# PEER mixture layers: where ScalarE copies the later quarters' gates, and how VectorE lays out its second-key one-hots

## The chip, the cores and the metric

One core of one Trainium2 chip runs the whole program. The metric is the device time of one execution in microseconds; the kernel before takes 3299.89 us (median of 3 runs, 3299.41 to 3300.56).

## The reference

Two transformer blocks in float32, one after the other, over 512 tokens of width 1024. Each has a mixer (gated linear attention in the first; retention and stick-breaking attention in the second) and then a PEER layer, and the change lies in the PEER layers alone:

```python
q = (ht @ w_query).reshape(T, 8, 2, 128)            # 8 heads, two halves
sub_scores = einsum('thpc,hpkc->thpk', q, sub_keys) # 128 keys in each half
top_s, top_i = top_k(sub_scores, 16)
cand = top_s[:, :, 0, :, None] + top_s[:, :, 1, None, :]
best_s, best_c = top_k(cand.reshape(T, 8, 256), 16)
expert_id = top_i[first] * 128 + top_i[second]      # one of 16384 experts
gate = softmax(best_s)
a = einsum('pd,ped->pe', x, expert_down[expert_id])
y = einsum('pe,ped->pd', gelu(a) * gate, expert_up[expert_id])
```

Each token so picks 128 experts (8 heads of 16), each with one row of a "down" table and one of an "up" table, 16384 x 1024 float32 each.

## The kernel before

The 512 tokens are four tiles of 128. Tiles 0 and 1 are gathered: GpSimd fetches each picked row with an indirect DMA (`fetch`, L2038) into rings of six buffers; VectorE multiplies and sums down rows (`score_rows`, L1843, its work on L1850) and adds up rows (`add_rows`, L1854, its work on L1870). Four rows for all 128 tokens are a unit. Tiles 2 and 3 are dense: the whole tables stream through SBUF in 128 blocks of 128 experts, one block for each value e of the first key. For block e TensorE computes the first product (`first_product`, L744, matmul on L750: 128 experts x 256 tokens), ScalarE the gelu of it (`block_gelu`, L1203, on L1208), VectorE multiplies two blocks by their gates (`weigh_pair`, L1793, on L1801), and TensorE accumulates the second product (`second_product`, L754, on L760). SyncE loads the blocks, four ahead, as the buffers come free.

The gates of the dense tiles are a table of experts x tokens, mostly zeros. They are built for four quarters of the first key in turn (32 values each), 256 tokens in 64 batches of 4 tokens for each quarter. For one batch, `gates_of_batch` (L770, matmuls on L786) multiplies a one-hot of the second key (128 picks x 128 keys for each token: `hits`, four buffers, in the memory called `levels`) with a one-hot of the first key times the gate in three bf16 parts (`hot`, in `x`): 12 matmuls of 128x32. The second-key one-hots come from ScalarE (`hit_batch`, L1210: four ACTIVATE on L1218, one on L1221) for all batches but the odd ones of the first quarter, which VectorE makes (`second_keys`, L1783, on L1789). `by_scalar` (L81) says which. VectorE makes the first-key side for 16 tokens at a time (`first_keys`, L1769, on L1777 and L1779). When 16 tokens (4 batches, one bank of PSUM; two banks take turns) are done, ScalarE copies the bank into the gate table in SBUF (`copy_gates`, L1223, on L1228).

The order of the work is written out by hand, for each engine in steps e = 0 to 127, and each engine runs strictly in its order. TensorE's step e (`dense_experts`, L800): first product of block e + 16 (from e = 8; the first 24 lie in the stage before), second product of e, then gate batches `batches_due(e - 1)` to `batches_due(e)` of the quarters 1 to 3. Before the steps stands the first quarter, with blocks 8 to 23 between its batches. ScalarE's step e is this:

```python
for u in range(units_due(e - 2), units_due(e - 1)):
    unit_gelu(layer, u)
if EARLY <= e + AHEAD - 1 < NKEY:
    block_gelu(layer, e + AHEAD - 1)
for n in range(batches_due(e) if e else 0, batches_due(e + 1)):
    hit_batch(layer, 1 + n // BATCHES, n % BATCHES)
for m in range(copies_due(e - 1), copies_due(e)):
    copy_gates(layer, 1 + m // WIDES, m % WIDES)
```

EARLY is 24 and AHEAD 16. First product e waits for the gelu of e - 2 (two banks). A copy waits for its four batches and for VectorE to have weighed the two blocks whose place it takes; a group of batches waits for the copy of the group two before it. VectorE's step e weighs blocks e + 4 and e + 5 if e is even, makes first-key sides up to `spreads_due(e)`, does a piece of the choice of experts for tile 1, and runs the units that a planner (`unit_table`) gives to the step.

Of the kernel before, what the change touches and what calls it, by code (L numbers as in the profile page):

```python
# [8 lines left out]
BF16 = mybir.dt.bfloat16  # L9
U32 = mybir.dt.uint32  # L10
I32 = mybir.dt.int32
ALU = mybir.AluOpType
# [3 lines left out]
P = 128  # L16
# [13 lines left out]
QA = NKEY // QUARTERS  # L30
UV = 4
BATCH = 4
# [9 lines left out]
HITS = 4  # L42
# [38 lines left out]
def by_scalar(q, n):  # L81

    return q > 0 or n % 2 == 0


def scalar_batches(layer, q, n):

    return sum(by_scalar(a, b) for a in range(QUARTERS) for b in range(BATCHES)) * layer \
        + sum(by_scalar(a, b) for a in range(q) for b in range(BATCHES)) + sum(by_scalar(q, b) for b in range(n))


def vector_batches(layer, q, n):

    return (layer * QUARTERS + q) * BATCHES + n - scalar_batches(layer, q, n)
# [7 lines left out]
LATER = (QUARTERS - 1) * BATCHES  # L102


def batches_due(e):

    return 0 if e < 0 else min(LATER, 2 * e + 4 + min(8, e // 4))
# [6 lines left out]

def copies_due(e):

    return 0 if e < 0 else min(LATER // 4, e // 2 + 3, batches_due(e + 1) // 4)


def blocks_before(n):  # L120
# [89 lines left out]
def build(nc, a, out, mod_dram, x_dram, two_pi):  # L210
    with ExitStack() as ctx:
        def sb(name, cols, dt=F32):
            return ctx.enter_context(nc.sbuf_tensor(name, [P, cols], dt))[:, :]
# [5 lines left out]
        ps = [psum[:, n * 512:(n + 1) * 512] for n in range(8)]  # L219
# [10 lines left out]
        modm = sb("mod", 6 * D)  # L230
# [8 lines left out]
        def part(base, at_kib, kib, dt=F32):  # L239
            v = base[:, int(at_kib * 256):int((at_kib + kib) * 256)]  # L240
            return v if dt == F32 else v.bitcast(dt)
# [25 lines left out]

        onehot = part(modm, 16, 3, BF16)
        wide_onehot = part(x_, 8, 4, BF16)
        row_at, row_to = part(modm, 16, 0.5), part(modm, 16.5, 0.5)  # L270
        cand = part(modm, 17, 0.5).rearrange("p (h n) -> p h n", h=2)
        place_no = part(modm, 19, 1, BF16).rearrange("p (k s) -> p k s", k=TOPK)
# [35 lines left out]
        second_no = part(hT_, 14, 0.5, BF16)  # L308
        hits = [part(lev_, b, 1, BF16) for b in range(HITS)]
# [47 lines left out]
        keyno16 = sb("key_numbers_16", P // 2).bitcast(BF16)  # L357
# [273 lines left out]
        def _(pe):  # L631
# [138 lines left out]
            def gates_of_batch(layer, q, n):  # L770

                m = (layer * QUARTERS + q) * WIDES + n // 4
                if by_scalar(q, n):
                    pe.wait_ge(hit_ready, scalar_batches(layer, q, n + 1))
                else:
                    pe.wait_ge(hit_by_vector, vector_batches(layer, q, n + 1))
                if n % 4 == 0:
                    pe.wait_ge(ga_ready, m + 1)
                    if q == 0 and n < 8:
                        pe.wait_ge(picks_copied, len(DENSE) * (layer + 1))  # L780
                    else:
                        pe.wait_ge(ga_copied, m - 1)
                for j in range(BATCH):
                    t = n % 4 * BATCH + j
                    for r in range(3):
                        last = nc.tensor.matmul(ps[6 + n // 4 % 2][:, t * QA:(t + 1) * QA], hits[n % HITS][:, j * P:(j + 1) * P],  # L786
                                                hot[n // 4 % 2][:, r, n % 4, :, j], start=r == 0, stop=r == 2)
                last.then_inc(ga_used, 1)

# [10 lines left out]
            def dense_experts(layer):  # L800

                for n in range(BATCHES):
                    gates_of_batch(layer, 0, n)
                    for e in range(blocks_before(n), blocks_before(n + 1)):
                        first_product(layer, e)
                for e in range(NKEY):
                    if EARLY <= e + AHEAD < NKEY:
                        first_product(layer, e + AHEAD)
                    second_product(layer, e)
                    for n in range(batches_due(e - 1), batches_due(e)):  # L810
                        gates_of_batch(layer, 1 + n // BATCHES, n % BATCHES)
                if layer == 0:
                    pe.wait_ge(x_ready, NT)
# [22 lines left out]
            for i in range(ALONE + 1):  # L836
                chunk(i)
                if i == 1:
                    pe.wait_ge(cst_in, 16 * 13)
                    for k in range(KC):  # L840
                        last = nc.tensor.matmul(ps[4][0:16, :], w_low[:, k, :], hT[:, k, :], start=k == 0, stop=k == KC - 1)
                    last.then_inc(low_done, 1)
                if i == 2:
                    seen.next(low_copied)
                    for c in range(2):
                        last = nc.tensor.matmul(ps[5 + c], w_up[:, c * P:(c + 1) * P], glow, start=True, stop=True)
# [93 lines left out]
            for h in range(8):  # L940
                prt = heads[h % 2]
                for j in range(NT):
                    n = h * NT + j
# [21 lines left out]
            for n in range(STICKS + LOOK):  # L965
                if n < STICKS:
                    h, j = n // NT, NT - 1 - n % NT
# [4 lines left out]
                if m >= 0:  # L972
                    h, j = m // NT, NT - 1 - m % NT
# [5 lines left out]
                    for i in range(NT - 1, j - 1, -1):  # L979
                        last = nc.tensor.matmul(bank[:, (i - j) * P:SEQ - j * P], sticks[:, 0 if i == j else 1, :],  # L980
                                                stay[h % 2][:, i, i * P:SEQ], start=False, stop=i == j)
# [12 lines left out]
        def _(act):  # L994
# [260 lines left out]
            def dense_acts(layer):  # L1255
# [16 lines left out]
                for e in range(NKEY):  # L1272
# [8 lines that stand above are left out]
                    if e and pieces_due(e - 2) <= EXP_PIECE < pieces_due(e - 1):  # L1281
                        gate_exp(1)
                    if layer == 0 and e and units_due(e - 2) < 2 * GROUPS + 1 <= units_due(e - 1):
                        seen.next(x_ready)
                        squares(0)
# [78 lines left out]
        def _(dve):  # L1364
            seen, step, chosen = Seen(dve), Chain(dve, c_dve), Chain(dve, c_top)
            picks, spreads = Chain(dve, c_picks), Chain(dve, c_first)
            n_out = [0]
            tt, ts, stt = nc.vector.tensor_tensor, nc.vector.tensor_scalar, nc.vector.scalar_tensor_tensor

            def spread(v, shape):  # L1370

                while len(v.shape) < len(shape):
                    v = v.unsqueeze(len(v.shape))
                return v.to_broadcast(shape)
# [200 lines left out]
            def by_head(v, n, width):  # L1575
                return v.rearrange("p (h n) -> p h n", n=width), [P, n, width]
# [5 lines left out]
            for t in range(NT):  # L1582
                hv, shape = by_head(hn[:, t, :], 8, P)
                step(tt(hv, hv, spread(rs[:, t * 8:t * 8 + 8], shape), ALU.mult))
                for m in range(2):
# [3 lines left out]
                    last = tt(half, half, sg1[:, m, t, :], ALU.mult)  # L1589
# [142 lines left out]
            def peer(layer):  # L1732
# [22 lines left out]
                finish_gates(0)  # L1755
                for g in range(WIDE // BATCH):
                    spreads(nc.vector.tensor_copy(key_rows[:, g], spread(keyno[:, 0:QA], [P, QA, BATCH])), 3)
                dve.wait_ge(picks_copied, len(DENSE) * (layer + 1))
                for q in range(QUARTERS):
                    spreads(ts(first_no[q], iaT, float(-q * QA), None, ALU.add), 3)  # L1760
# [22 lines left out]
                def second_keys(n):  # L1783

                    at = layer * QUARTERS * BATCHES + n
                    if at >= HITS:
                        dve.wait_ge(ga_used, at - HITS + 1)
                    shape = [P, BATCH, P]
                    tt(hits[n % HITS].rearrange("p (j k) -> p j k", j=BATCH), keyno16.unsqueeze(1).to_broadcast(shape),  # L1789
                       second_no[:, n * BATCH:(n + 1) * BATCH].unsqueeze(2).to_broadcast(shape), ALU.is_equal)\  # L1790
                        .then_inc(hit_by_vector, 1)

                def weigh_pair(e):  # L1793
# [10 lines left out]
                for n in range(BATCHES):  # L1804
                    if n % 4 == 0:
                        first_keys(0, n // 4)
                    if not by_scalar(0, n):
                        second_keys(n)
                    for u in range(first_units(n - 1), first_units(n)):
                        run_unit(layer, u)  # L1810
# [63 lines left out]
            def finish_tile(layer, t, y):  # L1874
# [6 lines left out]
                else:  # L1881
# [3 lines left out]
                    dve.wait_ge(out_ready, t + 1)  # L1885

            peer(0)
            dve.sem_inc(dve_to_act, 1)

# [40 lines left out]
            for m in range(2):  # L1930
                for t in range(NT):
# [8 lines left out]
                    r3, shape = by_head(r, 8, 64)  # L1940
# [5 lines left out]
            for h in range(8):  # L1946
# [3 lines left out]
                for j in range(NT):  # L1950
                    n = h * NT + j
# [24 lines left out]
            for n in range(STICKS + LOOK):  # L1976
# [3 lines left out]
                if n in (3, 6, 9, 12):  # L1980
                    seen.next(ss_done)
                    t = n // 3 - 1
# [6 lines left out]
                if n < STICKS:  # L1989
                    h, j = n // NT, NT - 1 - n % NT  # L1990
# [13 lines left out]
                if m >= 0:  # L2004
                    h, j = m // NT, NT - 1 - m % NT
# [13 lines left out]
            for t in range(NT):  # L2019
# [7 lines left out]
                rstd(1, D, t)  # L2027
                normed_tile(t, rows[:, 1, :], mod[:, 3, :])
            peer(1)


# [59 lines left out]
```

## Time and profile before

| | |
|---|---|
| median of 3 runs | 3299.89 us (3299.41 to 3300.56) |
| profiled execution | 3302.15 us, span 3300.2 us |
| mean granted TensorE clock | 0.973 |
| TensorE (matmul) busy | 3081.3 us, 93% |
| VectorE busy | 2418.4 us, 73% |
| ScalarE busy | 1338.2 us, 41% |
| GpSimd busy | 1304.0 us, 40% |
| DMA | 931.21 MB, mean 282 GB/s |

The span goes from the first to the last instruction; the execution's own time is 2 us longer. The two PEER layers' steps run from about 560 to 1570 us and from about 2240 to 3300 us. Engine names in the rows: PE is TensorE's matmul, PEld its weight load, DVE VectorE, ACT ScalarE, POOL GpSimd, SP SyncE. `L1208` is a line of the kernel.

### The profile page before, as it was taken

How to read it: one execution, taken by the hardware profiler on the slowest of the kernel's cores; microseconds unless marked ns; L12 is line 12 of the kernel's file. 1: busy time of each engine (PE TensorE's matmuls, PEld its weight loads, DVE VectorE, ACT ScalarE, POOL GpSimd, SP SyncE). 2: the span in 40 equal slices, each digit the busy share in tenths (PEclk: the TensorE clock that was granted, in tenths of full speed). 3: DMA queues.
4: the chain of work that ended last, by engine and by line, in shares of the span. 5: the costliest groups of instructions: out<-in, count | busy, mean ns of one | idle time of the engine just before them, and what ended most of it. 6: DMA issues, size and time to landing. Idle time of an engine off the chain costs nothing. (4 is left out here: it accounts for less than half of the span.)

```text
span 3300.2 us, 45872 instructions
## 1 busy us (share of the span) xinstructions
PE 3081.3 (93%) x16440; PEld 2052.6 (62%) x16440; DVE 2418.4 (73%) x5311; ACT 1338.2 (41%) x3417; POOL 1304.0 (40%) x1040
## 2 busy tenths in 40 slices
PE   7999899889999999999799999998899999999999
PEld 2466478756666666666344565687666666666664
DVE  5874459989889887877721243499898898888767
ACT  3232112676566555500101153126765656555100
POOL 0000000656665766666200000005465566777554
PEclk9999999999999999999899989999999999999999
DMA  8510252989999999999812101428899999999998
GB/s 293 193 42 36 96 209 79 339 291 395 379 380 395 403 409 409 409 409 409 314 56 83 36 35 39 179 77 296 283 391 375 370 398 400 409 408 409 409 409 336
DMA packets 282681, 931.21 MB, mean 282 GB/s; under 512 B 31804, under 2 KB 32460, under 8 KB 281944
## 3 DMA queue, kind: packets, MB, share of 16 engines
q0 software_dynamic: 147840, 536.96, 41.7%
q1 hardware_dynamic: 134616, 391.34, 31.4%
q8 instruction: 131, 2.15, 0.3%
q14 instruction: 94, 0.77, 0.1%
HBM read 921.87 MB, written 6.32 MB: 281 GB/s over the span
## 5 line engine op out<-in xcount | busy, mean ns | idle before, releaser
L750 PE MATMUL psum<-hT,mod 128*128 128x256 f32 x4096 | 966.7, 391 | 57.4 <-ACT big L1208 48.1
L750 PEld LDWEIGHTS psum<-hT,mod 128*128 128x128 f32 x4096 | 780.2, 195 | 182.9 <-issue 80.7
L1218 ACT ACTIVATE levels<-key_numbers,hT 128x128 bf16<-128x128 f32 x1792 | 566.9, 389 | 104.8 <-PE psum L786 104.0
L1870 DVE SCALAR_TENSOR_TENSOR tmp<-w,small,tmp 128x1024 f32<-128x1024 f32 x339 | 435.7, 1285 | 88.6 <-DMA w<-in_peer_v,tmp 43.5
L2045 POOL DMA_INDIRECT w<-in_peer_u,tmp x172 | 230.9, 1343 | 582.9 <-DVEq L1699 447.2
L1850 DVE CUSTOM_DVE_ANT_0 w<-w,hn 128x1024 f32<-128x1024 f32 x342 | 408.0, 1223 | 69.4 <-DMA w<-in_peer_u,tmp 33.9
L2045 POOL DMA_INDIRECT big<-in_peer_down,tmp x86 | 117.3, 1363 | 714.7 <-DVEq L1699 647.8
L760 PE MATMUL psum<-rows,big 128*128 128x512 f32 x768 | 343.9, 592 | 0.0
L786 PEld LDWEIGHTS psum<-x,levels 128*128 128x128 bf16 x6144 | 225.6, 101 | 170.0 <-issue 104.9
L1228 ACT ACTIVATE big<-psum 128x512 f32<-128x512 f32 x128 | 137.2, 1072 | 399.9 <-PE psum L786 390.1
L786 PE MATMUL psum<-x,levels 128*128 128x32 bf16 x6144 | 237.0, 196 | 54.9 <-DVE levels L1789 31.1
L1221 ACT ACTIVATE levels<-levels 128x512 bf16<-128x512 bf16 x448 | 282.2, 630 | 14.2
L2045 POOL DMA_INDIRECT w<-in_peer_down,tmp x170 | 225.9, 1329 | 143.6 <-DVE small L1850 102.7
L2045 POOL DMA_INDIRECT w<-in_peer_v,tmp x172 | 210.3, 1223 | 109.6 <-DVE tmp L1870 67.0
L1870 DVE SCALAR_TENSOR_TENSOR tmp<-big,small,tmp 128x1024 f32<-128x1024 f32 x169 | 217.2, 1285 | 43.8 <-DMA big<-in_peer_up,tmp 22.3
L2045 POOL DMA_INDIRECT w<-in_peer_up,tmp x170 | 203.1, 1195 | 115.0 <-DVE tmp L1870 76.0
L760 PEld LDWEIGHTS psum<-rows,big 128*128 128x128 f32 x768 | 145.9, 190 | 149.5 <-issue 145.4
L1850 DVE CUSTOM_DVE_ANT_0 big<-big,hn 128x1024 f32<-128x1024 f32 x170 | 203.8, 1223 | 30.1 <-DMA big<-in_peer_down,tmp 15.1
L1234 ACT ACTIVATE small<-small 128x4 f32<-128x4 f32 x128 | 26.0, 203 | 458.0 <-DVE small L1850 458.0
L760 PE MATMUL psum<-srow,big 128*128 128x512 f32 x384 | 172.6, 592 | 0.0
L760 PE MATMUL psum<-tmp,big 128*128 128x512 f32 x384 | 172.6, 592 | 0.0
L737 PE MATMUL psum<-hT,w 128*128 128x256 f32 x640 | 144.8, 379 | 0.0
(328 smaller groups left out, 4186.8 us busy)
## 6 DMA issues: line engine op xcount, KB each, us to landing
mod<-in_uT SPq DMA_DIRECT2D x256, 512.0 KB, 6.8
rows<-in_peer_v SPq DMA_DIRECT2D x64, 512.0 KB, 6.8
rows<-in_peer_up SPq DMA_DIRECT2D x64, 512.0 KB, 6.8
w<-in_w_in SPq DMA_DIRECT2D x14, 2048.0 KB, 7.8
srow<-in_peer_v SPq DMA_DIRECT2D x32, 512.0 KB, 7.0
tmp<-in_peer_v SPq DMA_DIRECT2D x32, 512.0 KB, 6.9
srow<-in_peer_up SPq DMA_DIRECT2D x32, 512.0 KB, 6.8
tmp<-in_peer_up SPq DMA_DIRECT2D x32, 512.0 KB, 6.9
```

The source lines that it names most:

```text
L737: last = nc.tensor.matmul(bank[:, 0:2 * P], w[:, k, c * P:(c + 1) * P], hT[:, k, tokens], start=k == 0, stop=k == KC - 1)
L750: last = nc.tensor.matmul(ps[4 + e % 2][:, 0:ND], ub[e % UV][:, k, :], hT[:, k, ND:SEQ], start=k == 0, stop=k == KC - 1)
L760: last = nc.tensor.matmul(y_dense[n][:, c * 512:(c + 1) * 512], zg(e)[:, n * P:(n + 1) * P], vb[e % UV][:, c * 512:(c + 1) * 512], start=e ...
L786: last = nc.tensor.matmul(ps[6 + n // 4 % 2][:, t * QA:(t + 1) * QA], hits[n % HITS][:, j * P:(j + 1) * P], hot[n // 4 % 2][:, r, n % 4, : ...
L1218: last = nc.scalar.activation(hits[n % HITS][:, j * P:(j + 1) * P], keyno, ACT.Abs, bias=nibT[:, n * BATCH + j:n * BATCH + j + 1])
L1221: nc.scalar.activation(hits[n % HITS], hits[n % HITS], ACT.Relu, scale=-1.0, bias=1.0).then_inc(hit_ready, 1)
L1228: nc.scalar.activation(gates[q % 2][:, :, 2 * m:2 * m + 2, :], ps[6 + m % 2].rearrange("p (j i a) -> p a j i", a=QA, i=8), ACT.Copy).then_ ...
L1234: nc.scalar.activation(g8[g % 2], a8[g % 2], ACT.Gelu).then_inc(act_out, 1)
L1850: nc.vector.tensor_tensor_reduce(out=row, in0=row, in1=hn[:, g // GROUPS, :], scale=1.0, scalar=0.0, op0=ALU.mult, op1=ALU.add, accum_out= ...
L1870: last = stt(y, row, c8[g % 2][:, b:b + 1], y, ALU.mult, ALU.add)
L2045: nc.gpsimd.indirect_dma_start(ring[n % ROWS], None, table, bass.IndirectOffsetOnAxis(idx[:, c:c + 1], 0))\
```

## The change

It does two things. The count of copies that ScalarE may have done by step e is taken from the batches of step e instead of e + 1. And VectorE's second-key one-hots, for the odd batches of the first quarter, are written key by key with the four tokens innermost, where they were token by token with the 128 keys innermost; for this a grid of key numbers, each four times, is written once in each layer, and TensorE reads the weights of these batches with a step of four elements.

```diff
 def copies_due(e):
-    return 0 if e < 0 else min(LATER // 4, e // 2 + 3, batches_due(e + 1) // 4)
+    return 0 if e < 0 else min(LATER // 4, e // 2 + 3, batches_due(e) // 4)
...
+        key_grid = part(modm, 16, 1, BF16).rearrange("p (k j) -> p k j", j=BATCH)
...
+                rows_of = "p (j k) -> p j k" if by_scalar(q, n) else "p (k j) -> p j k"
+                hit = hits[n % HITS].rearrange(rows_of, j=BATCH)
                 for j in range(BATCH):
                     t = n % 4 * BATCH + j
                     for r in range(3):
-                        last = nc.tensor.matmul(ps[6 + n // 4 % 2][:, t * QA:(t + 1) * QA], hits[n % HITS][:, j * P:(j + 1) * P],
+                        last = nc.tensor.matmul(ps[6 + n // 4 % 2][:, t * QA:(t + 1) * QA], hit[:, j, :],
                                                 hot[n // 4 % 2][:, r, n % 4, :, j], start=r == 0, stop=r == 2)
...
+                spreads(nc.vector.tensor_copy(key_grid, spread(keyno16, [P, P, BATCH])), 4)
...
-                    shape = [P, BATCH, P]
-                    tt(hits[n % HITS].rearrange("p (j k) -> p j k", j=BATCH), keyno16.unsqueeze(1).to_broadcast(shape),
-                       second_no[:, n * BATCH:(n + 1) * BATCH].unsqueeze(2).to_broadcast(shape), ALU.is_equal)\
+                    tt(hits[n % HITS].rearrange("p (k j) -> p k j", j=BATCH), key_grid,
+                       second_no[:, n * BATCH:(n + 1) * BATCH].unsqueeze(1).to_broadcast([P, P, BATCH]), ALU.is_equal)\
                         .then_inc(hit_by_vector, 1)
```

LATER is 192, the batches of quarters 1 to 3, and `batches_due(e)` is min(192, 2e + 4 + min(8, e // 4)).

## Rows read from the trace of the kernel before

**Rows 1.** The page: TensorE's busy line, and the chain that ended last.

```profile
PE 3081.3 (93%) x16440; PEld 2052.6 (62%) x16440; DVE 2418.4 (73%) x5311; ACT 1338.2 (41%) x3417; POOL 1304.0 (40%) x1040
...
DMA 9%; PE 2%; DVE 2%; POOL 2%; issue 1%; DVEq 0%; ACT 0%; POOLq 0%; ACTq 0%
```

**Rows 2.** Windows: from:to, length, busy time per engine, granted clock, DMA share, GB/s.

```profile
589.00:692.00 103.00, 86.52 (x1005) 75.13 (x1006) 100.57 (x174) 73.11 (x185) 67.65 (x52) 0.92 0.94 347
...
758.00:950.00 192.00, 177.51 (x1133) 122.76 (x1134) 162.74 (x358) 110.39 (x301) 113.59 (x91) 1.00 0.99 381
950.00:1100.00 150.00, 150.00 (x932) 102.54 (x931) 144.54 (x283) 94.02 (x249) 100.15 (x79) 1.00 1.01 394
1100.00:1500.00 400.00, 390.88 (x2189) 265.96 (x2188) 314.62 (x440) 176.06 (x479) 271.29 (x210) 0.99 1.03 409
2258.00:2361.00 103.00, 84.88 (x1009) 73.71 (x1010) 100.27 (x173) 73.22 (x186) 68.48 (x52) 0.95 0.95 351
...
2427.00:2620.00 193.00, 178.52 (x1131) 123.34 (x1130) 162.04 (x358) 109.71 (x299) 112.98 (x90) 0.99 0.98 376
2620.00:2800.00 180.00, 180.00 (x1123) 123.61 (x1122) 168.65 (x317) 111.79 (x297) 119.90 (x96) 1.00 1.02 398
```

**Rows 3.** Durations (ns, min/median/max) of L1789, L1777 and L1757, both layers.

```profile
L1789 DVE TENSOR_TENSOR levels<-key_numbers,hT x64: 680/689/693, 589.1 to 2359.5; 128x512 bf16<-128x512 bf16 x64
...
L1777 DVE TENSOR_TENSOR x<-x,hT x128: 405/421/448, 587.6 to 3059.9; 128x512 bf16<-128x512 bf16 x128
...
L1757 DVE CAST x<-key_numbers x8: 215/222/250, 583.7 to 2252.8; 128x128 bf16<-128x128 f32 x8
```

**Rows 4.** TensorE's waits (us, times, longest), first quarter of layer 1, then layer 2.

```profile
PE psum L786 <- DVE levels L1789: 14.9, 8, 2.9
PE psum L786 <- ACT levels L1221: 5.4, 3, 4.5
...
PE psum L786 <- DVE levels L1789: 16.2, 9, 2.2
```

**Rows 5.** Timeline of TensorE: first and last of L750's waits, each layer.

```profile
757.90 3.69 PE L750 MATMUL psum<-hT,mod 128*128 128x256 f32 x16 [1.49 <-ACT big L1208]
...
946.32 3.69 PE L750 MATMUL psum<-hT,mod 128*128 128x256 f32 x16 [1.09 <-ACT big L1208]
...
2426.67 3.69 PE L750 MATMUL psum<-hT,mod 128*128 128x256 f32 x16 [1.49 <-ACT big L1208]
...
2616.76 3.69 PE L750 MATMUL psum<-hT,mod 128*128 128x256 f32 x16 [1.09 <-ACT big L1208]
```

**Rows 6.** Timeline around one such wait: start, length, engine, line, [idle before].

```profile
790.08 0.93 PE L786 MATMUL psum<-x,levels 128*128 128x32 bf16 x24
...
790.66 1.05 ACT L1228 ACTIVATE big<-psum 128x512 f32<-128x512 f32 x1 [6.18 <-PE psum L786]
...
791.57 0.38 ACT L1208 ACTIVATE hT<-psum 128x256 f32<-128x256 f32 x1
791.84 1.27 ACT L1218 ACTIVATE levels<-key_numbers,hT 128x128 bf16<-128x128 f32 x4
...
792.10 3.69 PE L750 MATMUL psum<-hT,mod 128*128 128x256 f32 x16 [1.09 <-ACT hT L1208]
```

**Rows 7.** VectorE's waits: two rows of 760 to 1000, one of 950 to 1565.

```profile
DVE x L1777 <- PE psum L786: 20.2, 9, 4.2
DVE big L1801 <- ACT big L1228: 5.1, 1, 5.1
...
DVE tmp L1870 <- DMA w<-in_peer_v,tmp: 38.9, 49, 1.8
```

**Rows 8.** Weight loads: L786's durations, one batch in the timeline, L750's group.

```profile
L786 PEld LDWEIGHTS psum<-x,levels x6144: 95/101/117, 589.2 to 3080.5; 128*128 128x128 bf16 x199
...
654.11 0.54 PE L786 MATMUL psum<-x,levels 128*128 128x32 bf16 x12
...
L750 PEld LDWEIGHTS psum<-hT,mod 128*128 128x128 f32 x4096 | 780.2, 195 | 182.9 <-issue 80.7
```

## The prediction

> **What bounds the kernel now.** I read the page first. TensorE is busy 93% of the span, VectorE 73%, and the chain that ended last names DMA before any engine [rows 1]. So no single engine is the answer, and the stages have to be taken apart. The windows do that for the two mixture layers, which have the same shape [rows 2]. Four stretches matter in each.
>
> First quarter of the gates (589 to 692 us, and 2258 to 2361): VectorE is busy 100.6 of 103 us, TensorE 86.5. DMA moves 347 GB/s, under the 409 it reaches later. VectorE never waits here. TensorE does: 14.9 us in the first layer and 16.2 in the second on the one-hots of L1789, and some more on ScalarE's [rows 4]. VectorE is the bound, and the instruction TensorE waits for is the one that the diff rewrites.
>
> Later quarters, first part (758 to 950, and 2427 to 2620): TensorE is busy 177.5 of 192 us. Its gaps are all of one kind: L750, the first product of a block, waits for the gelu L1208. There are 13 such gaps in each layer, the first at 757.90 and the last at 946.32 in the first layer, 15.9 us together (0.69 to 1.49 each); in the second layer 13 from 2426.67 to 2616.76, 16.0 us [rows 5]. One of them in full [rows 6]: TensorE's gate products begin at 790.08; the copy L1228, which had waited 6.18 us for them, starts at 790.66 and takes 1.05 us; only behind it, in ScalarE's order, comes the gelu at 791.57, and the first product starts at 792.10, 1.09 us late.
>
> Then 950 to 1100: TensorE is busy all the time, at 394 GB/s. From 1100 to 1500 the queues move a flat 409 GB/s and VectorE waits for landed rows again and again (38.9 us on one form alone, 49 times, from 950 to the layer's end, none of it before 950) [rows 2, 7]. That last stretch is bound by DMA: it starts earlier if what is ahead of it ends earlier, but does not get shorter.
>
> **The change, part by part.**
>
> Copies. ScalarE's step e ends with the copies that `copies_due(e)` newly allows. Before, that was a batch count of step e+1 over 4; after, of step e. TensorE runs the gate batches up to `batches_due(e)` at its step e, after the second product. So before, a copy at ScalarE's step e could wait for the end of TensorE's step e+1, and the gelu of step e+1 behind it is wanted by TensorE at the start of its step e+2, that is, at once. I wrote out both functions for e = 0 to 127: they differ at e = 1, 3, 5, 7, 8, 10, 12, 14, 15, 17, 19, 21, 23, 24, 26, 28 and 30, so 17 of the 48 copies of a layer move one step later. From e = 32 on the other bound, e // 2 + 3, holds in both. First products lie beside second products only from e = 8: of the 17, that leaves 13, and two steps on from them comes a pattern of gaps 2, 2, 2, 1, 2, 2, 2, 2, 1, 2, 2, 2 steps. The 13 waits of the trace are spaced just so (two steps are about 17 us, one about 9.6). Each of these waits is one moved copy.
>
> After the change, the copy waits for TensorE's step e, and the gelus needed at its steps e+1 and e+2 are issued before it and one step behind it, 7 us before they are wanted. So all 15.9 and 16.0 us of gaps should go from TensorE. What moves behind other work is only the copy: ahead of it now stand the row gelus of a unit, one block gelu and 2 or 3 one-hot batches (1.27 us each on L1218 [rows 6] and a shorter pass on L1221), of which at most the last can still be running when TensorE ends its step. That makes a copy up to 2 us later than the products allow. TensorE needs the bank again only a group later, over 7 us on: covered. At a quarter's end VectorE waits for its last copy (5.1 us, once in a layer [rows 7]); that may grow to 7 us, beside 20.2 us that VectorE waits for TensorE in the same stretch: nothing. No DMA issue of SP or POOL is moved; both follow TensorE's and VectorE's progress.
>
> What is late next is DMA. From 758 to 1100 it moves 192 x 381 + 150 x 394 = 132,250 (us x GB/s). At 409 that takes 323 us, at 394 (what it reached while rows were already waited for) 336 us, against 342: the stretch can lose between 6 and 18.6 us, capped by the 15.9 of the gaps. Middle of 6 and 15.9: 11 us. In the second layer 193 x 376 + 180 x 398 = 144,210, which is 353 us at 409 and 362 at 398, against 373: between 10.7 and 16.0, middle 13 us. **Copies: 24 us** together (ends 17 and 32).
>
> One-hots. L1789 takes 689 ns for 128x512 bf16 with a stride of 0 innermost in one operand. The new form has both operands and the output with a unit stride innermost over four tokens, and the key dimension broadcast outside it. L1777, same operation, size and types, same pattern of its second operand, takes 421 ns [rows 3]. 32 instructions in each layer save 268 ns each: 8.6 us. Added is one copy of 512 elements per layer to fill the key grid, between 0.22 us (L1757, 128 elements) and 0.69 us; I take 0.5, in full, as TensorE's first gate batch waits for VectorE's chain there. That is 8.1 us a layer. VectorE fills this stage to 98%, so it counts in full, up to TensorE's own need (86.5 busy of 103, part of it at a granted clock of 0.92 [rows 2]). DMA would have to rise from 347 to 377 GB/s. **One-hots: 16 us** together; ends 0 (rows become the wait) and 20 (the gaps of ScalarE's one-hots shrink as well).
>
> The weights of TensorE's gate products now lie four elements apart in the odd batches of the first quarter: 384 loads in a layer. No row shows such a load. A batch of 12 loads and matmuls takes 0.54 us with the pipeline's fill, 24 take 0.93, so about 36 ns a pair; the moving operand is already read at that stride. The record of one load is 101 ns, that of an f32 load 195 [rows 8]. So the price lies between 0 and (195 - 36) x 384 = 61 us a layer, a gain being excluded because nothing gets denser. I take 0, from the moving operand. At 101 ns a pair it would be 25 us, of which some 20 are idle time of TensorE now.
>
> The Trainium skill (TensorE: Matmul & The Clock Gate, Weight-path perf modes) says that a fast weight load reads 32 bits at a time, two bf16 weights, which speaks against this change: two neighbours of the new order are not in one such word. The same table lists the read pattern as "packed or strided", which speaks for no cost. No row shows which holds, so the first reading is rival 5.
>
> **Sum.** 24 + 16 = 40 us from the profiled execution's 3302.15 us (span 3300.2): 3262. The median shown is 2.3 us lower, so 3260 us.
>
> **Rivals.**
> 1. DMA gives back most of the copies' gain. VectorE runs into row waits as soon as TensorE stops holding it, and the 409 GB/s stretch just starts with a longer backlog. For it: the margins above are 3% to 5%. Against: at 409 GB/s the first layer's rows 2 leave 16 us of DMA unused in the first quarter and 19 from 758 to 1100. Only the one-hots count: 3300 - 16 = 3284; with a little of the copies, 3276 to 3293. Chance 0.16.
> 2. More than forecast: all 32 us of gaps, 16 of one-hots, and some 8 us from a higher granted clock and fewer waits for ScalarE's one-hots. 3300 - 56 = 3244. Chance 0.12.
> 3. Slower: strided weight loads set TensorE's pace in the first quarter. Place: L786 in odd batches. It eats TensorE's 20 us of waits first, then works against the copies' 12 us: it decides from 32 / 384 = 83 ns over the present pair, near 120 ns. At the f32 load's 195 ns, 61 - 20 - 12 = 29 us a layer, 58 us more: 3358. Chance 0.05.
> 4. No change: both gains only turn into longer row waits, 3300. If DMA were the bound from the stage's start this would hold, but VectorE waits for no row before 950. Chance 0.06.
> 5. A strided pair takes twice as long, 72 ns for 36: 14 us a layer on TensorE, beside 20 us of its waits there. It costs the one-hots' gain at most, 3276. Chance 0.05. The Trainium skill's 32-bit reads, taken strictly, are this case.
>
> **How the numbers follow.** My own case, 3250 to 3275, has 0.56; with rivals 1, 2 and 5 that is 0.89 below 3293. A difference within 0.2% (6.6 us) is about what a measurement of this kernel cannot tell from none: 3293 to 3306, 0.06. Above: 0.05. The range reaches from rival 2 to most of rival 1: 3242 to 3288.
>
> **What would show it.** L1789's successor at about 421 ns, x64. The 13 waits of L750 for L1208 gone in both layers, and the copies still starting at the end of gate products but with no gelu queued behind. The first quarter down from 103 to about 95 us, L786's waits for it cut. TensorE's loads in odd batches still about 36 ns a pair. From 758 on, DMA near 400 GB/s, with VectorE's first row waits before 950. I am wrong if the stage after 1100 starts less than 12 us earlier in the first layer, if it starts earlier but ends no earlier, or if 12-matmul batches of L786 take over 1 us.

## The result and the profile after

The changed kernel takes 3254.49 us (median of 4 runs, 3254.21 to 3257.26), against 3300.22 us before on the same chip: a ratio of 0.986, interval 0.9848 to 0.9871, or 43 to 50 us. Forecast were 3260 us and a range of 3242 to 3288.

Both parts do what the diff says. The one-hots, from the view of single lines in the kernel after (duration min/median/max in ns), beside [rows 3]:

```profile
L1792 DVE TENSOR_TENSOR levels<-mod,hT x64: 417/422/427, 589.7 to 2329.3; 128x512 bf16<-128x512 bf16 x64
L1781 DVE TENSOR_TENSOR x<-x,hT 128x512 bf16<-128x512 bf16 x128 | 53.8, 420 | 15.9 <-PE psum L789 15.5
L1761 DVE COPY mod<-key_numbers x2: 412/416/419, 584.5 to 2229.6; 128x512 bf16<-128x512 bf16 x2
```

The second is the group of L1781, the old L1777: its twin to 2 ns. The third is the added key grid, 0.42 us a layer. TensorE's batches with the new stride of the weights take 0.57 to 0.58 us where they stand alone, against 0.54 to 0.56 before and 0.54 for the unchanged batches of the same kernel; one of them:

```profile
628.67 0.58 PE L789 MATMUL psum<-x,levels 128*128 128x32 bf16 x12 [2.01 <-DVE levels L1792]
```

The windows of the kernel after, the columns as in [rows 2]:

```profile
589.70:683.70 94.00, 80.46 (x980) 71.02 (x981) 91.69 (x174) 73.25 (x185) 67.43 (x51) 0.98 0.99 375
763.00:950.00 187.00, 187.00 (x1221) 129.07 (x1220) 171.57 (x377) 119.92 (x321) 127.60 (x97) 1.00 1.03 408
950.00:1100.00 150.00, 150.00 (x923) 102.88 (x922) 138.53 (x261) 86.09 (x223) 100.62 (x76) 1.00 1.01 397
1100.00:1500.00 400.00, 385.32 (x2087) 261.50 (x2086) 313.65 (x436) 165.99 (x450) 272.60 (x211) 0.99 1.03 409
2235.00:2330.00 95.00, 83.93 (x988) 73.53 (x989) 91.66 (x173) 73.01 (x185) 66.47 (x51) 0.95 0.98 373
```

The first quarter is down from 103 to 94 us with VectorE as full as before. The granted clock rose there in layer 1, from 0.92 to 0.98, and TensorE's busy time fell from 86.5 to 80.5 us; its idle time fell only from 16.5 to 13.5 us. But the stage is VectorE's, and in layer 2, where the clock stayed at 0.95, it got shorter as well. From 763 to 950 TensorE has no gap left, and DMA moves 408 GB/s where it moved 381. TensorE's waits in layer 1, first in the kernel before, then in the kernel after (us, times, longest):

```profile
PE psum L750 <- ACT big L1208: 23.2, 14, 4.6
PE psum L786 <- DVE levels L1789: 14.9, 8, 2.9
PE psum L786 <- ACT levels L1221: 10.3, 9, 4.5
PE psum L750 <- ACT hT L1208: 3.6, 3, 1.5
```

```profile
PE psum L751 <- ACT big L1211: 16.1, 7, 6.5
PE psum L789 <- DVE levels L1792: 13.3, 8, 2.0
PE psum L789 <- ACT levels L1224: 7.8, 4, 4.9
PE psum L751 <- ACT hT L1211: 1.3, 1, 1.3
```

The 13 waits of [rows 5] are gone. The waits for VectorE's one-hots are cut less: 14.9 to 13.3 us here, 16.2 to 10.3 in layer 2. The seven and one that L751 still has all come after 1140 us, the longest at 1194. They are of another kind, as the timeline there shows (idle before, in brackets):

```profile
1192.38 1.23 DVE L1853 CUSTOM_DVE_ANT_0 big<-big,hn 128x1024 f32<-128x1024 f32 x1 [0.69 <-DMA big<-in_peer_u,tmp]
...
1193.65 0.21 ACT L1237 ACTIVATE small<-small 128x4 f32<-128x4 f32 x1 [11.06 <-DVE small L1853]
1193.76 0.37 ACT L1211 ACTIVATE big<-psum 128x256 f32<-128x256 f32 x1
1194.27 5.38 PE L751 MATMUL psum<-hT,mod 128*128 128x256 f32 x16 [6.49 <-ACT big L1211]
```

ScalarE stands at the gelu of a unit, which VectorE has not scored because the rows land late, and the block's gelu stands behind it. This is where DMA takes back part of what the gaps gave: waits of this kind add up to 17.4 us in layer 1 and 16.9 in layer 2, where the kernel before has 10.9 and 13.5. VectorE's first waits for rows now lie before 950 us, where it had none; the longest group of them, from 560 to 950:

```profile
DVE tmp L1873 <- DMA w<-in_peer_v,tmp: 4.9, 13, 0.8
```

A copy in the kernel after, to be laid beside [rows 6]:

```profile
771.79 0.37 ACT L1211 ACTIVATE hT<-psum 128x256 f32<-128x256 f32 x1
...
774.72 0.93 PE L789 MATMUL psum<-x,levels 128*128 128x32 bf16 x24
...
775.49 3.70 PE L751 MATMUL psum<-hT,mod 128*128 128x256 f32 x16
775.72 1.07 ACT L1231 ACTIVATE big<-psum 128x512 f32<-128x512 f32 x1
776.58 0.42 ACT L1211 ACTIVATE hT<-psum 128x256 f32<-128x256 f32 x1
```

The gelu that the product at 775.49 wants was done at 772.2, before the copy. A gelu follows the copy still, at 776.58, but it is the next step's. The copy starts 1.0 us after the gate products began, 0.4 us later than in [rows 6], because one-hots stand before it: the "up to 2 us" of the prediction, and nobody waits for it.

Where the time went, from first and last starts of single lines in the traces (us; block 12 is the first whose second product reads its gelus from `big`, which the trace tells apart, at 778.5 us before and 763.2 after in layer 1):

| stretch | before, layer 1 / 2 | after | copies only | one-hots only | 4 early copies | 13 late copies |
|---|---|---|---|---|---|---|
| first gate product to last VectorE one-hot | 101.6 / 101.5 | 93.5 / 94.3 | 101.5 / 101.6 | 93.9 / 94.2 | 101.5 / 101.6 | 101.5 / 101.5 |
| to block 12's second product | 87.7 / 87.8 | 79.9 / 81.9 | 81.8 / 81.9 | 87.8 / 87.8 | 85.1 / 85.2 | 84.4 / 84.5 |
| to the last gate product | 632.8 / 633.2 | 622.0 / 621.1 | 621.6 / 621.2 | 636.7 / 633.8 | 634.7 / 634.9 | 621.6 / 622.0 |

The three stretches give 52 us together. The trace after is only 48 us shorter: the time from the last gate product to the last second product grew by 0.9 us in layer 1, that from there to layer 2's first gate product by 2.2 us, and the time ahead of layer 1's first gate product by 0.6. Apart from the key grid (0.42 us a layer, which lies ahead of the first gate product), the change touches nothing there. Yet the time between the layers is 636.2 to 637.1 us in all six traces of this document with the old one-hots, 639.2 to 640.0 in six of the eight with the new ones, and 636.9 and 637.4 in the other two. So some 2 us of the one-hots' gain seem to be lost there; by what is not shown.

### The profile page after: what moved, and what is told of

Its sections match the earlier page's. It is cut to its first block and busy times, and to the rows that moved or that the text cites. A ratio compares the mean times of both kernels' runs of the same rounds, so it can differ in the third digit from the quotient of the medians.

```text
span 3252.1 us, 45874 instructions
## 1 busy us (share of the span) xinstructions
PE 3070.5 (94%) x16440; PEld 2047.1 (63%) x16440; DVE 2400.6 (74%) x5313; ACT 1347.2 (41%) x3417; POOL 1339.4 (41%) x1040
## 5 line engine op out<-in xcount | busy, mean ns | idle before, releaser
L751 PE MATMUL psum<-hT,mod 128*128 128x256 f32 x4096 | 957.9, 388 | 35.4 <-ACT big L1211 32.1
L751 PEld LDWEIGHTS psum<-hT,mod 128*128 128x128 f32 x4096 | 773.9, 193 | 156.4 <-issue 57.1
L761 PE MATMUL psum<-rows,big 128*128 128x512 f32 x768 | 343.9, 592 | 0.0
L789 PEld LDWEIGHTS psum<-x,levels 128*128 128x128 bf16 x6144 | 227.5, 103 | 152.9 <-issue 102.7
L789 PE MATMUL psum<-x,levels 128*128 128x32 bf16 x6144 | 236.3, 196 | 40.1 <-DVE levels L1792 23.6
L2048 POOL DMA_INDIRECT w<-in_peer_v,tmp x172 | 218.1, 1268 | 98.4 <-DVE tmp L1873 54.3
L2048 POOL DMA_INDIRECT w<-in_peer_up,tmp x170 | 211.7, 1246 | 99.1 <-DVE tmp L1873 57.9
L761 PEld LDWEIGHTS psum<-rows,big 128*128 128x128 f32 x768 | 145.9, 190 | 149.6 <-issue 145.4
L761 PE MATMUL psum<-srow,big 128*128 128x512 f32 x384 | 172.6, 592 | 0.0
L761 PE MATMUL psum<-tmp,big 128*128 128x512 f32 x384 | 172.6, 592 | 0.0
```

The costliest lines, as they stand in the source:

```text
L751: last = nc.tensor.matmul(ps[4 + e % 2][:, 0:ND], ub[e % UV][:, k, :], hT[:, k, ND:SEQ], start=k == 0, stop=k == KC - 1)
L761: last = nc.tensor.matmul(y_dense[n][:, c * 512:(c + 1) * 512], zg(e)[:, n * P:(n + 1) * P], vb[e % UV][:, c * 512:(c + 1) * 512], start=e ...
L2048: nc.gpsimd.indirect_dma_start(ring[n % ROWS], None, table, bass.IndirectOffsetOnAxis(idx[:, c:c + 1], 0))\
```

## Experiments

The kernel before takes 3300 us on the chips of the first comparison and of the first four experiments, and 3350 to 3352 us on the chips of the other eight runs. So each kernel is held against the kernel before, or after, on its own chip.

**Each half alone, and the copies split in two.** From the kernel before, the first with the new `copies_due` only, the second with everything but it, and two that change it for some steps:

```diff
 e3: only steps before 8
-    ... batches_due(e + 1) // 4)
+    ... batches_due(e if e < 8 else e + 1) // 4)
 e4: only steps from 8 on
+    ... batches_due(e if e >= 8 else e + 1) // 4)
```

> The copies' half alone: later quarters' gates copied a step later, one-hots as before. Theory (two separate gains that add): 45.7 us less some 16 us of one-hots, so 30 us faster than before, near 3270 us; L750's 13 waits in each layer gone, L1789 still 689 ns. Rival (DMA is the common limit and each half alone would reach it): over 36 us faster, under 3264 us, and the two halves' gains sum to well over 46. Second rival (most of the gain is the one-hots'): 3285 us or more.

> The one-hots' half alone, copies as before. Theory: 8 us a layer, near 3284 us, with the first quarter's stage at about 94 us and L750's 13 waits a layer still there. Rival (common limit): 22 us or more faster. Second rival (VectorE's time turns into waits of the later stage): less than 8 us faster.

> Only the 4 copies of each layer before step 8 are moved (those of steps 1, 3, 5 and 7), nothing else. My prediction costed them at nothing: within 3 us of before. Rival: the stretch from the end of the first quarter to the first product's pairing got shorter by more than the 3 us of L750's two waits in it, so these four copies hold back ScalarE's one-hots: 3 to 5 us a layer, 6 to 10 us faster.

> Only the 13 copies of each layer from step 8 on are moved. Theory: all of the copies' gain, 28 to 32 us faster. Rival (DMA gives back a third and the early copies pay for it): 20 to 25 us faster. All 26 waits of L750 for the gelu gone in both cases, so what is missing from 32 us must show as VectorE's waits for rows or as later waits of L750.

| kernel | median us | ratio to before (interval) | gain us (interval) |
|---|---|---|---|
| before | 3301.19 | | |
| copies only | 3267.79 | 0.9899 (0.9883 to 0.9915) | 33 (28 to 39) |
| one-hots only | 3290.70 | 0.9962 (0.9946 to 0.9978) | 13 (7 to 18) |
| 4 early copies a layer | 3295.90 | 0.9984 (0.9975 to 0.9994) | 5 (2 to 8) |
| 13 late copies a layer | 3271.89 | 0.9913 (0.9897 to 0.9928) | 29 (24 to 34) |

The gains are worked out from the ratios; by the medians the one-hots alone win 10.5 us. Within these intervals the gains add: 33 and 13 are 46, the gain of the whole, and 5 and 29 are 34, for the 33 of the copies. The rival of a common limit falls: it wanted 22 us or more from the one-hots alone. So does the one that gives most to the one-hots, with 3285 us or more for the copies alone.

The early copies were costed at nothing (within 3 us) and are worth 5 us, between that and the rival's 6 to 10. TensorE's waits in layer 1 with only them moved:

```profile
PE psum L750 <- ACT big L1208: 24.2, 15, 4.6
PE psum L786 <- DVE levels L1789: 14.7, 8, 2.9
PE psum L786 <- ACT levels L1221: 8.3, 6, 4.5
```

The same waits for ScalarE's one-hots in the stretch to block 12 alone (690.8 to 778.5 us before, 688.2 to 773.3 with the early copies moved):

```profile
PE psum L786 <- ACT levels L1221: 4.9, 6, 1.3
```

```profile
PE psum L786 <- ACT levels L1221: 3.0, 3, 1.3
```

These 1.9 us are most of the 2.6 us by which the stretch gets shorter in each layer; the rest was not traced. In steps 0 to 7 TensorE has no first products, its steps mostly last 4 to 6 us, and ScalarE makes 2 or 3 one-hot batches in each. In the kernel before, ScalarE stands for TensorE at a copy in their midst (2.74 us at 716 us), with one-hots behind it:

```profile
715.16 0.93 PE L786 MATMUL psum<-x,levels 128*128 128x32 bf16 x24
...
716.13 1.08 ACT L1228 ACTIVATE big<-psum 128x512 f32<-128x512 f32 x1 [2.74 <-PE psum L786]
716.99 1.24 ACT L1218 ACTIVATE levels<-key_numbers,hT 128x128 bf16<-128x128 f32 x4
```

The late copies bring 29 of the 32 us of gaps. Two of the 13 gaps, 3.0 us, lie before block 12 (the stretch is 3.3 us shorter), the other eleven (13.0 us) shorten the next stretch by 11.2. DMA gives back little. The one-hots alone win 7.5 us in the first quarter of each layer and lose 3.9 and 0.6 before the last gate product. But the traced execution is the slowest of its seven (3296.41 us, the others from 3279.34), so that this loss may be the spread of the runs. L751 still has its waits there, 25.6 us in layer 1; that VectorE's lead only waits behind them is argued, not shown.

**All weight loads strided.** From the kernel after, ScalarE writes its one-hots in the new order too:

```diff
-                    last = nc.scalar.activation(hits[n % HITS][:, j * P:(j + 1) * P], keyno, ACT.Abs,
+                    last = nc.scalar.activation(hits[n % HITS].rearrange("p (k j) -> p j k", j=BATCH)[:, j, :], keyno, ACT.Abs,
...
-                rows_of = "p (j k) -> p j k" if by_scalar(q, n) else "p (k j) -> p j k"
+                rows_of = "p (k j) -> p j k"
```

> The kernel after, with ScalarE's one-hots laid out by key and then token as well, so that all 3072 gate weight loads of a layer, not 384, step over four elements. Theory (a strided load costs TensorE nothing): a batch of 12 still starts and ends in 0.54 to 0.55 us, pairs at 36 ns, and the whole is within 6 us of the changed kernel, near 3255 us. Rival (the load loses half its rate, 36 ns more a pair): 2688 more such loads a layer where TensorE is busy all the time, 97 us a layer, near 3440 us. A slower ScalarE write at this stride would show in L1218's successor, now 389 ns.

3273.73 us, a ratio of 0.9763 (0.974 to 0.9786) to before; the kernel after, on another chip where before also takes 3351 us, has 0.9765. So no time is lost that this interval, 8 us to either side, would show. The loads, then a step's 24 pairs, then ScalarE's writes:

```profile
L789 PEld LDWEIGHTS psum<-x,levels x6144: 110/118/135, 592.4 to 3059.9; 128*128 128x128 bf16 x199
...
1003.90 0.95 PE L789 MATMUL psum<-x,levels 128*128 128x32 bf16 x24
...
L1221 ACT ACTIVATE levels<-key_numbers,hT x1792: 532/553/622, 587.9 to 3050.2; 128x128 bf16<-128x128 f32 x200
```

One load's record is 118 ns instead of 101, but 24 pairs take 0.95 us instead of 0.93: about 1 ns a pair. The rival at half the load rate wanted 36 ns a pair and 3440 us, and falls. ScalarE, though, pays: 553 ns a write of 128 elements instead of 388. It has room for it here.

**DMA relieved.** The kernels before and after with half of each down block loaded, so that the products use stale values for the rest. The edit, the same in both:

```diff
-                sp.dma_start(ub[e % UV], layer_uT[layer][:, e * D:(e + 1) * D].rearrange("p (k n) -> p k n", k=KC))\
+                sp.dma_start(ub[e % UV][:, 0:KC // 2, :], layer_uT[layer][:, e * D:e * D + D // 2].rearrange("p (k n) -> p k n", k=KC // 2))\
```

> The kernel before with only half of each down block loaded (the first 4 of its 8 slices; the products use stale values in the rest), which takes 33.5 MB, 82 us at 409 GB/s, from each layer's queues and nothing from any engine. Theory (DMA binds after 1100 us only): the stretch from 1100 on gets shorter by what TensorE and VectorE wait for rows there, 10 to 40 us in all; the 26 waits of L750 stay. Rival (DMA binds everywhere): near 160 us less. It is the base for the next run.

> The kernel after with the same half loads. Theory (DMA gives back a few us of the gain, no more): the difference to the half-loaded kernel before is 45 to 56 us, a little above the 46 of the full kernels. Rival (DMA was what held the gain down, and the gaps of TensorE were worth more): over 60 us. Second rival (with DMA relieved the gaps were covered by something else): under 35 us.

3333.26 us (0.9934 of before, 0.9911 to 0.9958) and 3248.40 us (0.9685, 0.966 to 0.971): 85 us apart, outside the 45 to 56 of the theory. Against 46 us that would have spoken for the rival "DMA held the gain down". But the kernel before took 3352 us on this chip, so the sizes could not be compared before the next runs. What can be read by itself: relieved of 164 us of transfers (an estimate: 67 MB at the 409 GB/s of [rows 2]), the kernel before gains 19 us by the medians, 14 to 30 by the interval, so DMA does not bind everywhere. And in the half-loaded kernel after L751's waits for ScalarE are gone from layer 1 altogether (its whole list for L751, L761 and L789):

```profile
PE psum L789 <- issue: 10.3, 18, 1.6
PE psum L789 <- ACT levels L1224: 7.4, 3, 4.9
PE psum L789 <- DVE levels L1792: 6.2, 5, 1.6
...
PE psum L751 <- issue: 1.0, 3, 0.4
PE psum L761 <- DVE x L1804: 0.2, 1, 0.2
```

The full kernel after, on a chip where before also takes 3351 us (it comes next), still has them:

```profile
PE psum L751 <- ACT big L1211: 6.3, 3, 2.9
PE psum L751 <- issue: 5.6, 3, 4.4
```

All of them lie behind 1200 us. So they hang on the load of the queues, as waits for landed rows do. In the half-loaded kernel before the late ones are gone too: all that L750 waits for L1208, 15.9 us, lies before 1000 us.

**Both kernels again, on a chip where the kernel before is slower.** Unchanged kernels:

> The kernel before, unchanged, for a profile beside the other three of this job. The half-load kernels ran on a chip on which the kernel before took 3352 us instead of 3300, so their difference (85 us) cannot be laid beside the 46 us. If this chip is like that one, this trace shows what is longer there; if it is like the first, the segment times of the first trace should come back within 3 us.

> The kernel after, unchanged, beside the others. Theory (the size of the gain depends on the chip through the waits between engines): on a chip where the kernel before takes 3350 us, 80 to 95 us faster, as the half-load pair was; where it takes 3300, 44 to 48. Rival (the half loads made the gain larger): 44 to 50 us on either.

Before: 3350.45 us. After: 3271.73 us, 0.9765 (0.9751 to 0.9778) of the kernel before, 74 to 83 us less. The difference of the half-loaded pair, 85 us, is near the 79 us that the full pair has where the kernel before takes 3351: most of what lies between 46 and 85 comes with the chip, and at most a few us with the relief of DMA. The stretches of the kernel before are here 108.2, 94.7 and 651.4 us in layer 1, against 101.6, 87.7 and 632.8; of the kernel after 99.0, 85.0 and 620.7. The last is no longer than on the first chip: there it is the kernel before that loses. The windows of this last stretch, layer 1, first the kernels before and after on the first chip, then the same two here:

```profile
778.50:1411.30 632.80, 613.89 (x3849) 421.20 (x3849) 540.44 (x954) 362.36 (x975) 414.45 (x323) 0.99 1.01 397
763.20:1385.20 622.00, 613.27 (x3848) 421.50 (x3847) 542.86 (x969) 364.05 (x966) 423.95 (x323) 0.99 1.02 406
791.60:1443.00 651.40, 624.51 (x3848) 426.10 (x3847) 542.63 (x957) 363.41 (x974) 405.63 (x325) 0.98 0.99 386
775.70:1396.40 620.70, 613.24 (x3847) 421.05 (x3846) 543.36 (x968) 361.97 (x967) 422.37 (x324) 0.99 1.02 406
```

Of the 18.6 us that the kernel before loses in it, 8.0 are idle time of TensorE (26.9 for 18.9), and 10.6 are the same products taking longer, at a granted clock of 0.98 for 0.99. The timeline of one of its gaps, TensorE and ScalarE:

```profile
829.67 1.31 PE L786 MATMUL psum<-x,levels 128*128 128x32 bf16 x36
...
833.15 1.06 ACT L1228 ACTIVATE big<-psum 128x512 f32<-128x512 f32 x1 [5.11 <-remote]
834.01 0.41 ACT L1208 ACTIVATE hT<-psum 128x256 f32<-128x256 f32 x1
...
834.57 1.83 PE L750 MATMUL psum<-hT,mod 128*128 128x256 f32 x4 [3.59 <-issue]
```

The products end at 831.0, the copy starts 2.2 us later, with no releaser that the trace knows, and TensorE stands for 3.59 us, where the longest of the 13 gaps on the first chip was 1.49. The first four products behind it take 1.83 us, 0.46 each, and the whole 16 take 5.38 us for the 3.69 of [rows 6]: behind this gap TensorE ran for a while at the lower of its two clock levels. ScalarE's idle time in layer 1 lists copies with no known releaser (the time is all that it stood before them, not the delay alone):

```profile
ACT big L1228 <- PE psum L786: 184.8, 35, 11.1
ACT big L1228 <- remote: 91.5, 19, 7.7
```

In the kernel before on the first chip there is not one of that kind, nor in the kernel after or in the four experiments above. The changed kernel has such copies on this chip too:

```profile
ACT big L1231 <- remote: 46.5, 10, 7.0
```

Yet its TensorE has no wait at all from 760 to 1000 us. A late copy costs TensorE its lateness when a wanted gelu stands behind it, and the slower products behind a long gap as well; in the changed order it costs nothing there. That fits the larger gain; what delays the hand-over on these chips stays open, and so does how much of the 50 us that the kernel before loses here is due to it. The first two stretches are longer here in both kernels.

**A version that is faster still.** In steps 0 to 7 DMA has room (339 GB/s from 683.7 to 763 us in the kernel after). From the kernel after, `SHORT_UNITS` is raised, so that steps 0 to 7 take one or two units of gathered rows more, and the steps behind them fewer:

```diff
-SHORT_UNITS = 5
+SHORT_UNITS = 6   (e12: 7)
```

> The kernel after with SHORT_UNITS 6 instead of 5: one more unit of gathered rows is run in steps 0 to 7, where DMA moved 339 GB/s and VectorE waited 6.7 us for TensorE. Theory (from there on the queues are full, so 2.1 MB moved forward save up to 5 us a layer): 4 to 10 us faster than the changed kernel, 3245 to 3250 us. Rival (VectorE's extra 5.2 us delay its first-key one-hots or its weighing, and TensorE waits for them): no faster or some us slower.

> SHORT_UNITS 6 again, now with the kernel after beside it. Theory: the stretch from the end of the first quarter to the second product of block 8 keeps its length (80 to 82 us) and the rest of the layer gets 2 to 3 us shorter, 4 to 8 us in all. Rival: no difference beyond 3 us.

> SHORT_UNITS 7: two units more in steps 0 to 7 than in the kernel after. VectorE has 68.7 of 79.3 us busy there, a unit costs it 5.2 us. Theory: its room is just used up, so 3 us more than with 6 at best, and as likely nothing. Rival: VectorE becomes the bound, and TensorE waits for its one-hots and weighing: slower than with 6 by up to 5 us a layer.

The first run with 6 has 0.9718 (0.9698 to 0.9738), on the chip of the strided kernel, where the kernel after was not run. On one chip: 3271.73 us with 5, 3263.50 (0.9742, 0.9729 to 0.9755) with 6, 3257.11 (0.9718, 0.9705 to 0.9731) with 7. The interval of 6 touches both others, so that its 8 us are not certain, nor that 7 is faster than 6. The interval of 7 lies clear of that of 5: about 15 us faster than the changed kernel, more than the 3 us beyond 6 "at best" that were expected, and my rival, VectorE as the new bound, falls. (Block 8 in the expectation of the second is a slip for block 12; that stretch is 83.0 us with 6 for 85.0 with 5, not the same, as expected.)

The traces of 5 and 7 are only 8.4 us apart; the one is of an execution faster than its median (3269.44 us), the other the slowest of its five (3260.79). And 4.5 of the 8.4 lie ahead of layer 1's first gate product, where the kernels are the same. From there on, 7 against 5, in layer 1 and layer 2: the first quarter is 3.1 and 5.1 us longer, although its program is the same too; the stretch to block 12 is 2.5 us shorter and 0.9 longer; the one to the last gate product 1.5 and 0.1 us longer; and from there to the last second product it is 5.8 and 6.3 us shorter, 202.1 and 203.7 for 207.9 and 210.0. The stretches in which the two programs differ thus give 6.8 and 5.3 us, 12 of the 15. Windows of nearly all of this last stretch in layer 1, with 5 units and then with 7, show VectorE with fewer rows left to do (146.1 and 138.9 us busy):

```profile
1396.00:1597.00 201.00, 194.68 (x636) 118.10 (x633) 146.10 (x181) 10.24 (x36) 112.87 (x95) 0.99 1.02 404
```

```profile
1394.00:1589.00 195.00, 192.67 (x623) 116.85 (x620) 138.93 (x175) 10.23 (x35) 114.34 (x91) 1.00 1.02 406
```

So with 7 what is won is won at the far end. With 6 the far end does not show it (210.0 and 208.1 us to the last second product), so that this rests on one trace, and why the first quarter was longer stays open. More than 7 was not tried.

## Why the prediction was right, point by point

- What bounds each stage held. VectorE filled the first quarter, and the 268 ns an instruction came off it nearly whole: 8.1 and 7.2 us in the two layers, for 8.6. The key grid lies ahead of this stretch; taken at 0.5 us, it is 0.42.
- The 13 waits in each layer were the moved copies, as their spacing said, and are gone with them: L750 has not one wait between 760 and 1000 us with the copies alone moved.
- "Copies: 24 us" was too small: 33 us. Two steps of it failed. The copies of steps 1, 3, 5 and 7 were left out of the sum because L750 has no waits there; 5 us of the total are theirs, for the most part through ScalarE's one-hots, whose waits (4.9 us in that stretch) stood only in a rival, and without this cause. And I took the middle between two rates of DMA, 11 and 13 us of 15.9 and 16.0. DMA kept up better, at 408 GB/s from 763 to 950, and the late copies brought 29 of 32 us. The lower rate of 394 that I took as a bound was no limit of DMA, as the 408 shows; more likely it was TensorE's pace, as TensorE has no idle time from 950 to 1100 in either kernel (394 and 397 GB/s), but this was not tested.
- "One-hots: 16 us" was a little high: 13, interval 7 to 18. The stage gave 15; the 2 us that were longer between the layers would account for the rest.
- The sum was 40 us for 46 measured: the term of the copies was undersized by 9 us, and the one-hots, oversized by 3, hide a part of it. That the sum came so close is to that extent luck.
- Strided weight loads cost next to nothing, as taken from the moving operand: about 1 ns a pair, now shown over all 3072 loads of a layer. Of the rule of the Trainium skill (TensorE: Matmul & The Clock Gate, Weight-path perf modes) it is the pattern "packed or strided" that the traces bear out; the reading by 32-bit words that would have halved the rate they do not.
- Rival 1, DMA giving back most, is seen in part only: L751's late waits of 17.4 and 16.9 us in the two layers, against 10.9 and 13.5 before in the same part.
- Rival 2 had 8 us for a higher granted clock and fewer waits for ScalarE's one-hots. Those waits fell from 20.8 to 16.3 us over both layers; the clock rose in the first quarter of layer 1, where it did not set the stage's length.

## What to carry to other kernels

On an engine that runs in order, ask of each instruction that waits for another engine what is queued behind it and who wants that at once. Here the cure for 32 us of gaps was to issue the same copy behind a gelu and some one-hots, at no cost in work. And where an engine fills a stage, look for an instruction of its own with the same operation and size but a faster operand pattern: its row gives the price of the new form.

## What was not expected

- TensorE reads bf16 weights four elements apart at next to no cost in throughput (0.95 against 0.93 us for 24 pairs), while ScalarE writing 128 bf16 elements at that step takes 553 ns instead of 388.
- The same two kernels are 46 us apart on one chip and 79 on another. Copies that start late, by nothing that the trace shows (2.2 us in the one followed here), stand in both kernels there; behind them TensorE waits in the kernel before, and from 760 to 1000 us not once in the one after. An order with slack at its hand-overs was here also the steadier one.
- Two units of rows moved into the first steps shortened, in the one trace there is, the last 210 us of the dense blocks by 6 us a layer.
